# Layer 1's mixer: where the vector engine's modulation operations stand among the low parts, the convolutions and the output projection

## The reference, cut to what matters

```python
c_act = jax.nn.silu(c)
mod = c_act @ w_ada[l] + b_ada[l]                     # 2048 x 12288 weights for one row
sh1, sc1, gt1, sh2, sc2, gt2 = jnp.split(mod, N_MOD, axis=-1)
h = modulate(rmsnorm(x, g_norm_mix[l]), sh1, sc1)
proj = h @ w_in[l]                                    # 2048 x 3072
xr = causal_dwconv(xr, w_conv[l], b_conv[l])          # 4 taps over 1024 channels
hr = rg_lru(xr, ...)                                  # gates, then a scan over the tokens
y_pool = pool_mixer(xp, w_pool[l], ls_pool[l])
y = jnp.concatenate([y_lru, y_pool], axis=-1) @ w_out[l]
x = x + gt1[:, None, :] * y                           # then the feed-forward part, which needs sh2, sc2, gt2
```

## Time and profile before

| | |
|---|---|
| median of 3 runs | 2635.07 us (2633.29 to 2635.34) |
| the profiled execution's own time | 2635.05 us |
| its span, first to last instruction | 2633.4 us |
| PE busy | 2513.3 us (95%) |
| DVE busy | 1805.9 us (69%) |
| split part of the input projection | 173.95 to 270.82 us |
| output projection on PE | 270.82 to 390.0 us |
| last `ada_sum` of layer 1 | 395.67 us |

### The profile page before, as it was taken

One profiled execution on the slowest core, in us unless ns is written; L12 is line 12 of the kernel. 1 busy time (PEld: TensorE's weight loads), 2 busy tenths in 40 slices (PEclk: granted clock), 3 DMA queues, 4 the chain that ended last, 5 costly groups with the idle time before them and its releaser, 6 DMA issues.

```text
span 2633.4 us, 33569 instructions
## 1 busy us (share of the span) xinstructions
PE 2513.3 (95%) x13086; PEld 2121.3 (81%) x13086; DVE 1805.9 (69%) x1774; ACT 1080.1 (41%) x1244; POOL 222.2 (8%) x397
## 2 busy tenths in 40 slices
PE   4869999999999999999999998898999999999999
PEld 3659547888888888889999997787888888888887
DVE  6866766887888888678675446865678655555565
ACT  2025105444334344464336555444543344444443
POOL 4411220111111111001110000000001000000000
PEclk8889999999999999999999999999999999999999
DMA  9988895888888888648875554244578655555554
GB/s 367 366 318 295 310 384 175 313 327 319 314 308 318 307 313 293 197 159 292 310 270 162 162 170 132 81 144 151 201 259 307 218 190 189 189 189 189 187 191 144
DMA packets 290569, 638.97 MB, mean 243 GB/s; under 512 B 21754, under 2 KB 34556, under 8 KB 290076
## 3 DMA queue, kind: packets, MB, share of 16 engines
q1 hardware_dynamic: 233808, 432.22, 48.4%
q0 software_dynamic: 56096, 205.02, 21.0%
q10 hardware_dynamic: 556, 0.18, 0.0%
HBM read 635.28 MB, written 2.10 MB: 242 GB/s over the span
## 4 chain that ended last, share of the span: by engine, by line
PE 83%; DVE 8%; DMA 4%; issue 2%; ACT 2%; POOL 0%; DVEq 0%; ACTq 0%; POOLq 0%
PE PS L1627 82%; DMA R<-in_w_ada 4%; DVE R L973 2%; DVE WLO L954 1%; ACT WHI L511 1%; DVE R L1521 1%; PE PS L1848 1%; PE PS L1769 0%; DVE R L1349 0%; ACT R L584 0%; DVE R L1047 0%; DVE R L1590 0%; DVE YF L1592 0%; DVE R L1374 0%; DVE H L1120 0%
## 5 line engine op out<-in xcount | busy, mean ns | idle before, releaser
L954 DVE TENSOR_TENSOR WLO<-RAW,WHI 128x1024 fp32r<-128x1024 f32 x760 | 929.2, 1225 | 683.3 <-ACT WHI L511 681.0
L511 ACT ACTIVATE WHI<-RAW 128x1024 fp32r<-128x1024 f32 x760 | 804.3, 1060 | 1150.1 <-PE PS L1627 1146.5
L1627 PE MATMUL PS<-WHI,H 128*128 128x512 f32 x3296 | 1027.8, 393 | 32.3 <-issue 18.9
L1627 PEld LDWEIGHTS PS<-WHI,H 128*128 128x128 f32 x3296 | 618.4, 189 | 164.8 <-issue 28.5
L1627 PE MATMUL PS<-WLO,H 128*128 128x512 f32 x1648 | 645.0, 391 | 0.0
L973 DVE SCALAR_TENSOR_TENSOR R<-R,CA 128x1024 f32<-128x1024 f32 x360 | 461.3, 1281 | 70.4 <-DMA R<-in_w_ada 63.2
L1627 PE MATMUL PS<-H,WHI 128*128 128x256 f32 x2656 | 490.9, 287 | 12.8 <-DVE WLO L954 11.7
L1627 PEld LDWEIGHTS PS<-H,WHI 128*128 128x128 f32 x2656 | 417.8, 193 | 19.1 <-DVE WLO L954 16.4
L1627 PE MATMUL PS<-WHI,HID 128*128 128x512 f32 x1280 | 395.8, 390 | 0.0
L1627 PE MATMUL PS<-H,WLO 128*128 128x256 f32 x1328 | 377.6, 284 | 0.0
L1627 PEld LDWEIGHTS PS<-WLO,H 128*128 128x128 f32 x1648 | 311.5, 189 | 65.9
(11 more groups left out here) (215 smaller groups left out, 1266.7 us busy)
## 6 DMA issues: line engine op xcount, KB each, us to landing
R<-in_w_ada POOLq DMA_DIRECT2D x384, 512.0 KB, 6.6
RAW<-in_w_in SPq DMA_DIRECT2D x88, 1024.0 KB, 5.9
RAW<-in_w_ffn_in SPq DMA_DIRECT2D x88, 1024.0 KB, 5.0
RAW<-in_w_ffn_gate SPq DMA_DIRECT2D x44, 1024.0 KB, 6.3
RAW<-in_w_ffn_up SPq DMA_DIRECT2D x44, 1024.0 KB, 5.2
RAW<-in_w_ffn_down SPq DMA_DIRECT2D x44, 1024.0 KB, 8.2
RAW<-in_w_ffn_out SPq DMA_DIRECT2D x44, 1024.0 KB, 5.1
RAW<-in_w_out SPq DMA_DIRECT2D x32, 1024.0 KB, 5.1
```

Of the source, the lines that this page charges most:

```text
L511: nc.scalar.activation(WHI[j][:, :, :], RAW[slot][:, 2 * half:2 * half + 2, :], ACT.Copy)\
L954: nc.vector.tensor_tensor(WLO[j][:, :, :], RAW[slot][:, 2 * half:2 * half + 2, :], WHI[j][:, :, :].bitcast(F32), ALU.subtract).then_inc(lo ...
L1627: return nc.tensor.matmul(o, a, b, start=start, stop=stop, skip_group_check=True)
```

## The change

Four things are moved; nothing is computed differently.

- DVE does the low parts of s = 0 and 1 ahead of the first operations, and 12 operations stand there where 16 did.
- One convolution follows each low part of s = 2 to 9, where two followed each of s = 1 to 4. `gates(0)` and `gates(1)` now wait for the half of the convolutions that each reads.
- The loop over s has 22 operations where it had 24: one at s = 7, then two at s = 11, 13, ... 23 and one at s = 10, 12, ... 22. So 34 operations are done by the end of the loop where 40 were, and 62 stand behind it where 56 did (8, 26, 10, 8, 10).
- PE's gates, `ada_sum`s and ACT's sigmoids and exponentials are placed by the new order; one `ada_sum` leaves the input projection for half unit 1 of the output projection.

```diff
-ADA_BEFORE, ADA_IN_W_IN = 16, 24
-SUM_IN_W_OUT = {7: 6, 16: 7, 23: 8, 30: 9}
+ADA_BEFORE = 12
+ADA_IN_W_IN = {s: (s == 7) + (s >= 10) + (s in range(11, 24, 2)) for s in range(2, 24)}
+ADA_FIRST = ADA_BEFORE + sum(ADA_IN_W_IN.values())
+SUM_IN_W_OUT = {1: 5, 10: 6, 18: 7, 25: 8, 31: 9}
...
-                if s in (9, 11, 13, 15):
-                    sigmoids((s - 9) // 2)
-                if s in (16, 17):
+                if s in (9, 12, 14, 16):
+                    sigmoids((9, 12, 14, 16).index(s))
+                if s in (17, 18):
...
-                if n >= 5 and kt == 6:
+                if n >= 5 and kt == 8:
                     ada_end()
...
+            lo(2)
             for _ in range(ADA_BEFORE):
                 ada_rest()
-            for s in range(24):
+            for s in range(2, 24):
                 lo()
-                if 1 <= s < 5:
-                    convolution(2 * (s - 1))
-                    convolution(2 * (s - 1) + 1)
-                ada_rest()
+                if s < 10:
+                    convolution(s - 2)
+                for _ in range(ADA_IN_W_IN[s]):
+                    ada_rest()
...
-            for _ in range(24):
+            for _ in range(26):
                 ada_rest()
             residual_of(0, 15, 3)
...
-            for _ in range(len(ADA_REST) - ADA_BEFORE - ADA_IN_W_IN - 50):
+            for _ in range(len(ADA_REST) - ADA_FIRST - 52):
                 ada_rest()
...
+                if n < 2:
+                    pe.wait_ge(conv_step, 12 * (n + 1))
                 if n == 0:
-                    pe.wait_ge(conv_step, 24)
...
-            group("A", kind="T", quads=Q_WIN1, then={3: lambda: ada_sum((ACC, G)[0]), 7: lambda: gates(0)})
-            group("B", then={1: lambda: gates(1), 3: lambda: gates(2), 5: lambda: gates(3)})
+            group("A", kind="T", quads=Q_WIN1, then={7: lambda: gates(0)})
+            group("B", then={2: lambda: gates(1), 4: lambda: gates(2), 5: lambda: ada_sum((ACC, G)[0]),
+                             6: lambda: gates(3)})
             group("A", then={0: lambda: windows(0), 2: lambda: windows(1), 4: lambda: pool_products(0),
-                             5: lambda: ada_sum((ACC, G)[1]), 7: lambda: pool_products(1)})
+                             7: lambda: pool_products(1)})
```

More of the change, by code:

```diff
@@ L759, in _ @@
                     copy_out("A", tiles(20, 4))
-                if s in (9, 11, 13, 15):
-                    sigmoids((s - 9) // 2)
-                if s in (16, 17):
+                if s in (9, 12, 14, 16):
+                    sigmoids((9, 12, 14, 16).index(s))
+                if s in (17, 18):
                     act.wait_ge(c8_done, 1)
                     act.wait_ge(rg_sig, 8)
-                    for t in range(4 * (s - 16), 4 * (s - 16) + 4):
+                    for t in range(4 * (s - 17), 4 * (s - 17) + 4):
                         nc.scalar.activation(R[:, t, :], R[:, 32 + t, :], ACT.Exp, scale=SM[:, t:t + 1])\
```

## The result

The changed kernel takes 2640.42 us in the median (2636.36 to 2642.97, 20 runs), the kernel before 2634.8 us (2630.28 to 2636.54, 20 runs). The ratio is 1.0021, with a 95% interval from 1.0014 to 1.0027: slower by 5.6 us. The prediction had 2634.0 and no measurable change as the likeliest, so it was wrong in the side. The profiled execution has a span of 2639.1 us, 5.7 more than before.

A forecast was written before the change was run, and what follows sets the result against it. It took PE to be busy 95% of the span, with waits set by DVE's loads on full queues. Terms of -13.1, +2.4 and +9.7 us gave -1.0, so 2634.0 us, 80% range 2626 to 2642, no measurable change at 0.58.

The forecast's parts named there:

- The start: Opening up to `gates(0)`: low part of s = 2 starts at 172.2, half units end at 192.3, 13.1 us earlier.
- the rival in which a late restart costs 2 us: Opening: loads restart slowly after DVE's blocked time, X is 11 and the sum +1, inside the forecast; no chance of its own.
- X: How much earlier PE reaches `gates(0)` and then the output projection: 13.1 us, with bounds of 18 and 8.
- What counts is that 12 and not 18 operations stand ahead of s = 2: Opening: doing s = 0 and 1 early is worth nothing by itself; fewer operations ahead of s = 2 bring the gain.
- PE from the gates to the output projection: Input projection after `gates(0)`: again 65.4 us without a gap, nothing charged, output projection starts at 257.7.
- slower, 2642: Rival, chance 0.18: DVE lacks tiles in the input projection's second half, PE waits, 9 us lost, sum +8.
- The recurrence: DVE's row behind the last low part: 2.4 us later against PE, line 1362 4.3 us ahead of the output projection.
- The output projection: Six more operations, 3.15 MB, and about 0.65 MB of a unit at 390 GB/s cost 9.7 us.
- The PE waits that arise do not add: Output projection: PE waits 6 us at group 8's sum, ends units at about 127, last operation ends at 136.9.
- The sum: Whole kernel: -13.1 + 2.4 + 9.7 = -1.0 us against the profiled execution, 2634.0.
- the upper bound of 14.8 us: Six moved operations at 2.07 us each, 12.4, plus the recurrence's 2.4; paired with X = 8 it gives +7.
- The lower end: Best-case pairing: X of 18 with six moved operations at 1.34 us each, 8.1, gives -10.

The follow-up runs named there:

- run 2: Changed kernel with six opening operations ahead of the low parts of s = 0 and 1 and six behind, not all twelve behind: 2627.39 us.
- run 8: Changed kernel with the opening of before (16 operations, low part, operation, low part, operation), 56 operations behind the loop: 2635.98 us.
- run 5: Changed kernel with 28 operations in the loop (two after each low part from s = 10), so 56 behind it: 2633.96 us.
- run 6: Changed kernel with six operations ahead of the first low parts and six behind, and 28 operations in the loop: 2620.46 us.
- run 10: Changed kernel with six operations ahead of the first low parts, 28 in the loop, and group 5's bias six operations later: 2619.15 us.
- run 9: Changed kernel with six operations ahead of the low parts, 28 in the loop, six inside the recurrence, group 5's bias six operations later: 2616.25 us.
- run 3: Changed kernel with six modulation tiles of group 8 loaded in only 128 of 1024 columns, all operations still done: 2637.69 us.
- run 11: Changed kernel with the output projection's 16 unit loads cut to a quarter, all products still made: 2631.21 us.
- run 12: Changed kernel with the 48 tiles of groups 7 to 9 loaded at an eighth, all operations still done: 2617.12 us.
- run 1: Changed kernel with PE taking group 8's sum at half unit 28 of the output projection, not 25: 2640.55 us.

## Why the prediction was wrong

**"The start": 13.1 us foretold, 10.7 measured.** PE at s = 0 (158.1), the row of two low parts (148.48) and the six gapless half units came as described (175.72 to 194.72 is 19.0 us; 6 x 2.79 + 2.1 is 18.8). What failed is the step "I put the landing at 147.9 ... seven more follow at 2.04 us". The unit landed at 147.4, but the low part of s = 2 came at 174.35 and not at 172.2: the fifth operation began 1.0 us later than foretold, and the eight from there took 16.8 us, not 15.6. The stream that restarts after 19.5 us without an issue has 2.22 us from operation to operation (157.60 to 173.15), not the 2.04 that I took from the steady stream. This was named as the rival in which a late restart costs 2 us, and measured so (X 10.7, named as 11). What I never asked is what the blocked time costs against another order of the same instructions: 10 us by run 2.

**"What counts is that 12 and not 18 operations stand ahead of s = 2" was wrong as the main cause**, though not in the sum. Run 8 has the old opening and 18 operations ahead of s = 2, and the same `gates(0)` but for 3.3 us. So of the 10.7 us 1.8 came from the `ada_sum` that left this stretch, at most 5 from the convolutions spread over eight half units, 0.5 from run 8's earlier start, and 3.3 from the opening: two half units done early (5.6), less a low part that came 2.2 us later than run 8's first (172.12) with four fewer operations ahead of it. Run 2 shows what twelve operations ahead of s = 2 give when DVE does not stand blocked: 10.9 us more.

**"PE from the gates to the output projection": right.** 65.4 us foretold, 65.4 measured, without a gap, and the queues at 311 GB/s (325 estimated). The rival "slower, 2642" had the right time by the wrong mechanism, and that is luck: DVE got its tiles there, and even 28 of them with 0.5 to 0.8 us lost (runs 5 and 6). Its mechanism shows a little in the other two kernels with 28, as 0.7 and 2.6 us of waits on PE (runs 10 and 9).

**"The recurrence": 2.4 us foretold, 4.2 measured.** The order term was right (line 1365 starts 4.7 us ahead of the output projection, foretold 4.3, before 6.7). I left out that the eight operations in the middle also wait for loads: they took 12.7 us in the trace of before (270.97 to 283.67) and now 14.9 (262.21 to 277.13), with 2.17 us of waiting before the last. In the trace of before DVE had stood 4.44 us at the bias ahead of the last low part, in which buffers could fill; the change took that sum away. That this wait was what had filled them is argued, not shown.

**"The output projection": 9.7 us foretold, 12.0 measured; the step whose mechanism failed.** It missed by 2.3 us, as the start did by 2.4. I priced the six moved operations by their bytes on queues at 390 GB/s, with some of a unit's bytes given back: 9.7 us. They cost 12.0, near the 12.4 that I had used only as an upper bound, 2.07 us for each operation. Run 5 confirms it from the other side: six operations fewer, 11.6 us less. In the eleven kernels with full-size loads the stretch from the resumption to the last sum, divided by its operations, is 2.02 to 2.13 us, be they 42, 48 or 54. Runs 3, 11 and 12 show that the bytes misled: 2.75 MB less gave 3.1 us, and half of SP's bytes less gave 9.7 (111.42 to 101.75), where 6.7 MB at 358 GB/s would be 18.7. A way to write the pace that fits is this: a tile buffer's turn is issue, landing and operation, and four buffers share it. With the landings of the changed kernel and of run 11, (6.5 + 1.28 + 0.5) / 4 = 2.07 and (5.8 + 1.28 + 0.5) / 4 = 1.9, where 0.5 is POOL's issue; measured were 2.06 and 1.88. While DVE uses each tile at once this holds almost by definition, since the landing was measured in the same stretch and contains the waiting on the queues. It doesn't say what sets the landing, and it fails in run 12 (1.27 against 1.70). The prediction had worked out this very number (2.05, for the input projection) and did not use it for the end. How the landing itself divides into the tile's own bytes, the other three tiles and the units isn't settled: to cut the units to a quarter takes 0.7 us from it, to cut the tiles to an eighth 3.2. The Trainium skill (DMA: Bandwidth & Descriptors, Anatomy of one DMA) has 2.0 us plus bytes over 436 GB/s, which gives as an estimate 3.2 us for 512 KB and 2.15 us for 64 KB. For the six short tiles of run 3 the trace is near it (median 2.4 us), for those of run 12 less so (3.3); for 512 KB with four in flight no run's median is (5.8 to 6.7 us).

**"The PE waits that arise do not add": right**, by run 1, but with less room than foretold. Group 8's last operation came 109.9 us into the stage, not 104.8, so the wait at its sum was 10.0 us and not 6; PE ended its units 136.8 us into the stage, not 127; and ahead of the last sum it waited 4.16 us, not 9 or more.

**The sum.** -10.7 + 4.2 + 12.0 = +5.5 where -13.1 + 2.4 + 9.7 = -1.0 was foretold. All three terms were off to the same side, and the upper bound of 14.8 us for the last two (16.1 measured) did not hold both. The lower end was not added up right either: -18 + 8.1 leaves out the 2.4 us of the recurrence that the upper end has, and with them it is -7.5. Of the signs named beforehand, the last sum at 401.1 lies outside 389 to 400, as a wrong prediction was to show itself. Run 5 also gives the limit of the whole idea: with the six operations back in the loop the changed kernel is as fast as the one before, not faster, because the blocked opening eats what the order gains. Runs 2, 6 and 9 take that away and are faster than the kernel before by 0.2, 0.5 and 0.7%.

## What to carry to other kernels

Price an operation that is moved behind the last independent work by the pace of its stream as the trace shows it: the time between two ends over the number of operations, 2.02 to 2.13 us here. For a stream through N buffers that is near the turn (issue, landing and use, over N) as long as the loads are the same; with other sizes of load read it anew. Don't put an instruction that waits for a load ahead of instructions that would drain the buffers: run 2 does as many operations before the same point and gains 13 us in the medians, because DVE works while the unit lands and so POOL's next loads start 11 us sooner (140.64, not 151.80). And when an operation is moved, look where the sums and biases that follow it come to stand, but measure before you mend it: three of the variants (runs 5, 6 and 8) met a sum 4 to 5 us early, and taking that wait out of run 6 gained nothing that could be measured (run 10).

## What the runs showed of the hardware

A consumer that stands blocked costs the loads that it would have set off. In the 10.55 us in which DVE did nothing the four tiles under way still landed (141.1 to 147.0 us) and the queues moved 399 GB/s from 138 to 144 us; but POOL's next issue came 9.9 us later than before, from 149 to 152 us the queues moved 45 GB/s, and the low part of s = 2, twelve operations later, came 10 us late (run 2). A short wait need not cost that: 4 us of it in the recurrence made no difference that could be measured (runs 6 and 10). A 64 KB tile takes 3.3 us in the median where eight times as many bytes take 6.5. And halving SP's bytes behind the resumption speeds the tile stream by 9% only (2.06 to 1.88 us). The granted clock was 0.79 from 354 to 386.6 us in the changed kernel, around PE's wait of 10.02 us: 48 products took 23.48 us behind it and 20.85 in runs 5 and 6, which have no such wait. DVE, whose last operation ended the stage, waited for PE nowhere in that stretch.
